# First attention: VectorE's maxima reordered, the scale moved into the rope tables

## What is computed

```python
# part A: 8 query heads, 2 key/value heads, head width 64
qa = apply_rope(rms_norm(qa, a_q_norm_g), ang_a)
ka = apply_rope(rms_norm(ka, a_k_norm_g), ang_a)
p = softmax(qa . ka * scale)               # scale = 64 ** -0.5
out_a = p . va
# part B: 4 heads of two softmaxes each, value width 128
p = softmax(qb . kb * scale)               # (head, 2, query, key)
w = p[:, :, 0] - lam * p[:, :, 1]
out_b = rms_norm(w . vb, subln_g) * (1.0 - lam_init)
x = x + concatenate([out_a, out_b]) . w_out
```

## Time and profile before

| | us |
|---|---|
| median of 3 runs | 2621.97 |
| lowest, highest | 2620.18, 2624.56 |
| the profiled execution, its own time | 2624.35 |
| its span, first to last instruction | 2622.5 |
| busy: TensorE matmul, VectorE, ScalarE, GpSimd | 2486.1, 1751.2, 961.3, 379.5 |
| first maximum of the first attention | at 179.76 |
| first maximum of its last job | at 349.86 |

### The profile page before, as it was taken

One profiled execution on the slowest core, in us unless ns is written; L12 is line 12 of the kernel. 1 busy time (PEld: TensorE's weight loads), 2 busy tenths in 40 slices (PEclk: granted clock), 3 DMA queues, 4 the chain that ended last, 5 costly groups with the idle time before them and its releaser, 6 DMA issues.

```text
span 2622.5 us, 37978 instructions
## 1 busy us (share of the span) xinstructions
PE 2486.1 (95%) x13765; PEld 2129.2 (81%) x13765; DVE 1751.2 (67%) x3865; ACT 961.3 (37%) x1723; POOL 379.5 (14%) x353
## 2 busy tenths in 40 slices
PE   8997779999999988999989999999999999999998
PEld 6766678777778966794588989999899989999987
DVE  5526556554236556557899986878878787877765
ACT  3325532222223545511255553333333333333332
POOL 1000220110000000100000012333233333332300
PEclk9999989999999998999999999999999999999999
DMA  4110004663222210022024477888878888887764
GB/s 186 65 49 1 1 1 179 223 236 124 81 96 81 81 41 40 1 81 89 17 73 169 169 265 246 311 281 283 276 266 281 289 280 274 285 284 258 263 200 153
DMA packets 123511, 431.43 MB, mean 165 GB/s; under 512 B 11696, under 2 KB 36528, under 8 KB 111168
## 3 DMA queue, kind: packets, MB, share of 16 engines
q1 hardware_dynamic: 74768, 241.20, 26.5%
q0 software_dynamic: 47520, 186.14, 20.2%
q10 hardware_dynamic: 1040, 1.67, 0.2%
HBM read 399.61 MB, written 29.36 MB: 164 GB/s over the span
## 4 chain that ended last, share of the span: by engine, by line
PE 77%; DVE 13%; ACT 3%; issue 3%; DVEq 2%; DMA 1%; ACTq 1%; SPq 0%
PE ps L2224 19%; PE ps L2197 17%; PE ps L1950 10%; PE ps L1903 7%; PE ps L1806 5%; PE ps L1989 5%; PE ps L2183 4%; PE ps L2259 2%; DVE r L1649 1%; PE ps L2122 1%; ACT r L700 1%; PE ps L1874 1%; PE ps L2067 1%; DVE r L1645 1%; PE ps L2132 1%
## 5 line engine op out<-in xcount | busy, mean ns | idle before, releaser
L2197 PE MATMUL ps<-hd_hi,uT_hi 128*128 128x384 f32 x1024 | 349.9, 342 | 0.8 <-ACT uT_lo L951 0.7
L2197 PE MATMUL ps<-hd_hi,uT_lo 128*128 128x384 f32 x1024 | 346.6, 338 | 0.0
L2197 PE MATMUL ps<-hd_lo,uT_hi 128*128 128x384 f32 x1024 | 346.5, 338 | 0.0
L2224 PE MATMUL ps<-v_hi,ew_hi 128*128 128x512 f32 x768 | 319.7, 416 | 3.9 <-DVE ew_lo L1622 3.4
L2224 PE MATMUL ps<-v_hi,ew_lo 128*128 128x512 f32 x768 | 303.6, 395 | 0.0
L2224 PE MATMUL ps<-v_lo,ew_hi 128*128 128x512 f32 x768 | 301.4, 392 | 0.0
L1602 DVE TENSOR_TENSOR uT_lo<-ps,uT_hi 128x512 fp32r<-128x512 f32 x204 | 140.7, 690 | 146.6 <-ACT uT_hi L924 146.5
L924 ACT ACTIVATE uT_hi<-ps 128x512 fp32r<-128x512 f32 x256 | 152.3, 595 | 192.9 <-PE ps L2183 192.8
L2197 PEld LDWEIGHTS ps<-hd_hi,uT_lo 128*128 128x128 f32 x1024 | 192.6, 188 | 11.0
L2197 PEld LDWEIGHTS ps<-hd_hi,uT_hi 128*128 128x128 f32 x1024 | 192.8, 188 | 9.6 <-ACT uT_lo L951 1.3
L596 POOL DMA_INDIRECT big<-peer_u,r x128 | 145.6, 1137 | 334.1 <-DVE r L1706 310.3
(11 more groups left out here) (352 smaller groups left out, 5205.0 us busy)
## 6 DMA issues: line engine op xcount, KB each, us to landing
big<-wst SPq DMA_DIRECT2D x70, 1024.0 KB, 4.9
r<-peer_u SPq DMA_DIRECT2D x128, 512.0 KB, 6.8
r<-peer_v SPq DMA_DIRECT2D x128, 512.0 KB, 4.8
r<-wada POOLq DMA_DIRECT2D x48, 512.0 KB, 4.7
gd<-big POOLq DMA_DIRECT2D x24, 1024.0 KB, 8.7
big<-gd SPq DMA_DIRECT2D x32, 768.0 KB, 9.6
x<-x_in SPq DMA_DIRECT2D x4, 512.0 KB, 6.5
xd<-x SPq DMA_DIRECT2D x4, 512.0 KB, 10.3
```

The lines of the kernel that those rows point to most:

```text
L2197: mm = pe.matmul(ps[:, acc_bank(j), 0:DN], w[:, k, :], h[:, KD // 2 * half + k, :], start=(half == 0 and k == 0 and i == 0), stop=(half == ...
L2224: mm = pe.matmul(ps[:, 2 + 2 * t + half, :], w[:, P * t:P * t + P], vv[:, 512 * half:512 * half + 512], start=(i == 0 and n == 0), stop=(i ...
```

## The change

Four edits. The scale of the scores is multiplied into the rope tables of the queries. The maximum is negated by the reduction itself, the multiply behind it goes, and the exponential has no scale. VectorE's loop calls the maxima through `job_max(i)`, at another place: in a pair of single heads the second head's maximum comes first, ahead of `meta_probs` and `head_out` of earlier jobs, and `finish_probs` of the pair's first head goes behind these; behind a double head the next job's maxima come right behind `finish_probs`, ahead of `meta_probs` and `head_out`; behind the second single head of a pair they stay behind `head_out`. And ScalarE's `sub_square` runs one job later.

```diff
-                               ps[:, 2 * (s % 2):2 * (s % 2) + 2, 0:HALF], ACT.Exp, scale=SCALE,
+                               ps[:, 2 * (s % 2):2 * (s % 2) + 2, 0:HALF], ACT.Exp,
                                bias=sst[:, 1, s:s + 1], accum_out=sst[:, 2, s:s + 1])
...
-                if i >= 2:
-                    sub_square(i - 2)
-
+                if i >= 3:
+                    sub_square(i - 3)
+
+            sub_square(NPV - 2)
             sub_root(0, T - 1)
...
-                    v.tensor_tensor(rope[:, 2 * kind + sw], ropec[:, 2 * (kind // 2) + sw],
-                                    each(ropeg[:, 2 * kind + sw, :], 5), ALU.mult)
+                    v.scalar_tensor_tensor(out=rope[:, 2 * kind + sw], in0=ropec[:, 2 * (kind // 2) + sw],
+                                           scalar=1.0 if kind % 2 else SCALE, in1=each(ropeg[:, 2 * kind + sw, :], 5),
+                                           op0=ALU.mult, op1=ALU.mult)
...
             def score_max(s):
                 v.wait_ge(s_ready, s + 1)
-                v.tensor_reduce(sst[:, 0, s:s + 1], ps[:, 2 * (s % 2):2 * (s % 2) + 2, 0:HALF], AX.XY, ALU.max)
-                v.drain()
-                v.tensor_scalar(sst[:, 1, s:s + 1], sst[:, 0, s:s + 1], -SCALE, None, ALU.mult).then_inc(max_ready, 1)
+                v.tensor_reduce(sst[:, 1, s:s + 1], ps[:, 2 * (s % 2):2 * (s % 2) + 2, 0:HALF], AX.XY, ALU.max, negate=True)
+                v.drain().then_inc(max_ready, 1)
...
+            def job_max(i):
+
+                _, s, n, _ = pv_jobs[i]
+                for j in range(n):
+                    score_max(s + j)
+
+            job_max(0)
             for i in range(NPV + 2):
-                if i < NPV:
-                    _, s, n, _ = pv_jobs[i]
-                    for j in range(n):
-                        score_max(s + j)
-                if i < NPV:
+                scored = i + 1 < NPV and pv_jobs[i][2] == 1 and pv_jobs[i + 1][1] % 2
+                if scored:
+                    job_max(i + 1)
+                elif i < NPV:
                     finish_probs(i)
+                    if i + 1 < NPV and pv_jobs[i][2] == 2:
+                        job_max(i + 1)
                 if 1 <= i <= NPV:
                     meta_probs(i - 1)
                 if i == NPV + 1:
                     sub_norm(0)
                 if i >= 2:
                     head_out(i - 2)
+                if scored:
+                    finish_probs(i)
+                elif i + 1 < NPV and pv_jobs[i][2] == 1:
+                    job_max(i + 1)
             sub_norm(1)
```

## The result

The changed kernel takes 2638.36 us (median of 5, 2632.92 to 2640.08) against 2623.11 before: ratio 1.0055, 95% interval 1.0040 to 1.0069. It is 15 us slower. Forecast were 2627.0 and a range to 2634, so the direction of the sum was right and its size was not: the result lies above the range.

The account below looks back on a forecast made before the run. The first attention was taken as a round trip through three engines, none full. Full-clock steps +2.7, GpSimd contention -2.2 and low clock +4.5 made +5.0 on 2621.97: 2627.0 us, range 2617 to 2634 (8 in 10).

Parts of the forecast that it names:

- The walk at full clock: First attention, step by step without low clock: pairs -5.2, doubles +6.6 and -2.0, first pairs +3.3; sum +2.7 us.
- Late steps of doubles: Doubles whose transposes wait for `head_out` behind both maxima: step 5.33 instead of about 4.76, 11 times, +6.6 us.
- First steps of doubles: First double of each tile, transposes released in the singles' order: step 4.22 against 4.70, four times, -2.0 us.
- First pairs of a tile: First pair of singles after doubles, tiles 1 to 3: late releases twice, 6.9 against 5.78, +3.3 us.
- rival 1: TensorE's longer bursts keep the clock high; low stretches and tile 2's 1.4 us loss go: -0.9, 2621.1 us; chance 0.20.
- the term of the clock: Doubles: as much half-clock time as before, 16.9 us, now on the path at 0.36 each: +4.5 us, bounds 0 and 9.
- rival 2: Slower: clock low twice as long in doubles, +9.0 instead of +4.5, so 2631.5 us; chance 0.20.
- GpSimd beside VectorE: Combinations in doubles slowed by GpSimd's weight splits are partly hidden in the longer steps: -2.2 us, bounds 0 and -4.9.
- The negated maximum: Reduction negates, multiply goes: two maxima 0.85 apart, exponential some 0.1 sooner; 0.08 used in the first doubles.
- The square: Run a head later in ScalarE's idle time, keeping ScalarE from waiting for the later `head_out`: 0 us.
- Rival 3: Faster: `head_out` does not really hold the transposes, so doubles drop to 4.3 each: -12, 2610 us; chance 0.08.
- rival 4: Negation or order gains nothing in pairs, as ScalarE's copy delays the second exponential: the -5.2 goes, 2632 us; chance 0.07.

Follow-up runs that it names:

- the extra products: Changed kernel plus four 128x256 products in TensorE's idle time in late steps, output overwritten: 2618.49 us, ratio 0.9983 to before; with two products 2619.17.
- the small edits: Kernel before with only the negated maximum, the scale in the tables and the later square, VectorE's order unchanged: 2614.91 us, ratio 0.9973.

## Why the prediction was wrong

**The walk at full clock was right.** Pairs 5.33, measured 5.32. Late steps of doubles 5.33, measured 5.32 to 5.39 in nine of eleven where the clock was kept high (the others: 5.68, and 6.92 beside GpSimd). First steps of doubles 4.22, measured 4.05 clear of GpSimd. First pairs of a tile 6.9, measured 6.96 (271.17 to 278.13). Transposes at M + 2.36, measured M + 2.35. The whole stage, from first maximum to last job, takes 168.0 with the extra products (346.04 - 178.07) and 170.1 before, -2.1, where the sum without the clock was 2.7 - 2.2 = +0.5. The 2.6 between them are the 1.4 of tile 2's singles, 0.9 in the doubles and 0.7 in tile 0, less 0.3 in the other singles. The 1.4 the prediction gave to rival 1 alone; the changed kernel gained them although the clock of its doubles fell.

**The step that failed is the term of the clock**: "16.9 x 0.36 = 6.0, for three steps of four: +4.5, with as much time at the half level as before. Bounds: 0 [...] and twice as much, 9". Measured are 44.4 us at the half level, 2.6 times the 16.9, and 16.3 us for them. The price, 0.37 in the mean where 0.36 was worked out, agrees partly by luck. The working took a step that is all at the half level and 8.3 long. In the first three tiles there is none: the steps are 6.6 to 7.2, with the transposes and values alone at the half level, and cost 13.0 us for 30.9, 0.42 a microsecond. In the last tile it is 3.3 us for 13.5, 0.24, for one of its two steps is held by the combination beside GpSimd anyway (7.88, and 6.92 at full clock). The amount was what failed, and its upper bound with it, which was a round factor and came from no row. The reduction to three steps of four was wrong as well, for all of the low time lies in the late steps. Each late step with the longer rest now runs its transposes and values at the half level, then its scores at full; before it was some 3.4 us in a tile and 6.8 in the last. The prediction names a cause (one rest of 2.4 instead of two of 0.7 and 1.0) in its upper bound and in rival 2, and sizes it at twice. With the measured amount it is 2.7 - 2.2 + 16.3 = 16.8; less the 2.6 above this is the 14.2 by which the stage grew.

**GpSimd beside VectorE** was sized right. The combination at the end of tile 1 takes 1.88 in the changed kernel,

```profile
...
267.47 1.88 DVE L1203 SCALAR_TENSOR_TENSOR r<-r,coef 128x528 f32<-128x528 f32 x1
...
```

and its step is 264.30 to 271.17, 6.87, no longer than the others. With the extra products the two steps in tile 3 are 4.93 and 6.92 (328.86, 333.79, 340.71) where 4.07 and 5.33 are normal, together 2.5 of excess, against the 4.9 of the earlier trace rows: -2.4, with -2.2 predicted.

**The negated maximum** was undersized: 0.08 in the doubles, 0.19 measured. Alone, the small edits are worth 7 us of the median and 4.2 of the stage.

**The table products** take 0.48 each, as before them the plain ones; my 3.29 for eight was the span of eight overlapping instructions. They are hidden, as said.

**The square** was costed at 0 and said to protect ScalarE's exponentials. It does: without it they are 2.16 late. What that is worth depends on the clock: nothing that the median shows in the changed kernel, and 10 us with the extra products.

**The rivals.** Rival 1 (the clock stays high) is what the extra products make, and they land where it said: 2621.1 forecast, 2618.5 and 2619.2 measured. Unaided, the opposite happened. Rival 2 had the right term, more low clock in the doubles, with too small a size. Rival 3 falls by the timeline of the doubles, whose transposes follow `head_out`, and rival 4 by that of the pairs, which take 5.32.

## What to carry to other kernels

Moving an instruction ahead of another on one engine also moves everything behind it: ask for each semaphore behind the moved ones which in-order queue it holds, and what in that queue feeds the moved instruction itself. Here `head_out` held the transposes, and behind them stood the very scores that the early maxima need; put into the time in which VectorE waits anyway, the same instruction cost nothing and the order gained 23 us. When a change lets TensorE rest longer in one piece and puts it on the path at once, take the low clock for every step of that stretch as the bound, not a multiple of what it was. Here that bound would have been 11 x (8.3 - 5.33) = 33 us, and 16.3 were measured.

## What the runs showed of the hardware

Two extra products, 1.13 us together, in each of the late steps made the kernel 19 us faster, since TensorE then kept the full clock through the doubles; the same two in the kernel before took the half level from 16.9 to 3.6 us and left the length of the doubles as it was (76.2 and 76.3). And the clock and the steps locked together: in nine of the changed kernel's eleven late steps, eight of which take 6.6 to 6.9 us, the transposes and values run at 1.2 GHz and the scores at 2.4, time after time, where I had counted on stretches that fall anywhere. Some 3.4 us of each of these steps are at the half level.

A combination on VectorE (128x528, two inputs in SBUF) takes 0.77 us alone and 1.88 beside a split on GpSimd; the longest in the changed kernel took 3.63.
